# Down weights issued by ScalarE instead of SyncE in a hybrid decoder's mixture of experts

## The reference

```python
def moe_ffn(x, norm_ffn, w_router, b_router, w_gu, b_gu, w_down, b_down):
    xn = rms_norm(x, norm_ffn)
    logits = xn @ w_router + b_router
    top_v, top_e = lax.top_k(logits, 4)              # 4 of 32 experts
    gates = jax.nn.softmax(top_v, axis=-1)
    ...
    h = xn[tok] @ w_gu[e] + b_gu[e]                  # (rows, 1024) @ (1024, 2048)
    gate = jnp.minimum(h[:, :1024], 7.0)
    up = jnp.clip(h[:, 1024:], -7.0, 7.0)
    y = ((up + 1.0) * gate * jax.nn.sigmoid(1.702 * gate)) @ w_down[e] + b_down[e]   # (rows, 1024) @ (1024, 1024)
    ...
    return x + out                                   # y added at its tokens, times the gate
```

## Time and profile before

| | |
|---|---|
| median of 3 runs | 1318.44 us (1316.54 to 1318.85) |
| time of the profiled execution | 1316.15 us |
| its span | 1314.3 us |
| PE busy | 1235.2 us, 94% of the span |
| DMA, mean over the span | 352 GB/s |
| of the two queues of the run: issued by SP / by ACT | 460.42 MB / 1.05 MB |
| granted TensorE clock, mean | 0.993 |

### The profile page before, as it was taken

One profiled execution on the slowest core, in us unless ns is written; L12 is line 12 of the kernel. 1 busy time (PEld: TensorE's weight loads), 2 busy tenths in 40 slices (PEclk: granted clock), 3 DMA queues, 4 the chain that ended last, 5 costly groups with the idle time before them and its releaser, 6 DMA issues.

```text
span 1314.3 us, 17102 instructions
## 1 busy us (share of the span) xinstructions
PE 1235.2 (94%) x6632; PEld 576.2 (44%) x6632; DVE 350.1 (27%) x887; ACT 221.5 (17%) x479; POOL 16.6 (1%) x27
## 2 busy tenths in 40 slices
PE   7999999999899999899898989999999998989998
PEld 4556778766433433333332433333434333333332
DVE  2552455415461212111221212122111221211113
ACT  2123234300431111111111111011111111111110
POOL 0000000001100000000000000000000000000000
PEclk9999989999899999999999999999999999999999
DMA  9684642487369999999999999998999999999994
GB/s 334 174 247 151 227 126 73 105 289 297 128 269 429 429 428 428 427 429 429 428 428 429 428 428 428 428 377 356 429 427 430 429 428 428 430 428 428 430 427 201
DMA packets 76531, 462.15 MB, mean 352 GB/s; under 512 B 19282, under 2 KB 34370, under 8 KB 51650
## 3 DMA queue, kind: packets, MB, share of 16 engines
q1 hardware_dynamic: 71874, 460.42, 86.4%
q10 hardware_dynamic: 4608, 1.05, 0.4%
HBM read 458.48 MB, written 5.07 MB: 353 GB/s over the span
## 4 chain that ended last, share of the span: by engine, by line
PE 56%; DMA 39%; DVE 2%; ACT 2%; issue 1%; SPq 0%; DVEq 0%; ACTq 0%
DMA arena<-w_down 37%; PE banks L1241 12%; PE banks L1168 11%; PE banks L2027 6%; PE banks L585 5%; PE banks L527 2%; PE banks L763 2%; PE banks L1362 2%; PE banks L1198 2%; DMA arena<-w_gu 2%; PE banks L1147 1%; PE banks L1107 1%; PE banks L639 1%; PE banks L2046 1%; PE banks L544 1%; PE banks L652 1%
## 5 line engine op out<-in xcount | busy, mean ns | idle before, releaser
L1168 PE MATMUL banks<-arena 128*64 128x512 f32 x1984 | 442.5, 596 | 28.1 <-DMA arena<-w_gu 28.1
L1168 PEld LDWEIGHTS banks<-arena 128*64 128x64 f32 x1984 | 138.5, 137 | 303.8 <-issue 240.3
L1241 PE MATMUL banks<-arena 128*64 128x512 f32 x1056 | 236.4, 594 | 12.6 <-DMA arena<-w_down 12.5
L1298 DVE TENSOR_SCALAR arena<-banks 128x512 f32<-128x512 f32 x33 | 22.8, 692 | 475.2 <-PE banks L1168 446.7
L1241 PEld LDWEIGHTS banks<-arena 128*64 128x64 f32 x1056 | 73.7, 137 | 156.6 <-issue 121.1
L1271 ACT ACTIVATE arena<-arena 128x512 f32<-128x512 f32 x33 | 20.8, 630 | 542.0 <-DVE arena L1298 542.0
L1324 DVE TENSOR_TENSOR arena<-banks,arena 128x528 f32<-128x528 f32 x64 | 45.3, 708 | 176.6 <-PE banks L1147 176.6
L2027 PE MATMUL banks<-arena 128*128 128x512 f32 (+1 forms) x192 | 79.0, 569 | 0.0
L585 PE MATMUL banks<-arena 128*128 128x264 f32 x256 | 62.3, 398 | 0.5 <-ACT arena L804 0.5
L1147 PE MATMUL banks<-arena 128*128 128x264 f32 x256 | 61.2, 392 | 0.0
L1267 ACT COPY arena<-banks 128x512 f32<-128x512 f32 x33 | 19.3, 586 | 220.9 <-PE banks L1129 220.8
(11 more groups left out here) (348 smaller groups left out, 931.0 us busy)
## 6 DMA issues: line engine op xcount, KB each, us to landing
arena<-w_gu SPq DMA_DIRECT2D x128, 2048.0 KB, 23.9
arena<-w_down SPq DMA_DIRECT2D x64, 2048.0 KB, 24.7
arena<-w_in SPq DMA_DIRECT2D x8, 2048.0 KB, 11.3
arena<-cache_moba_k SPq DMA_DIRECT2D x16, 256.0 KB, 2.9
arena<-cache_moba_v SPq DMA_DIRECT2D x16, 256.0 KB, 2.7
arena<-w_out SPq DMA_DIRECT2D x2, 2048.0 KB, 12.7
arena<-w_in SPq DMA_DIRECT2D x2, 1024.0 KB, 9.2
arena<-cmp_w_k SPq DMA_DIRECT2D x1, 2048.0 KB, 10.4
```

Of the source, the lines that this page charges most:

```text
L1168: mm = nc.tensor.matmul(banks[64 * x:64 * x + 64, BG + b, :], xgT[:, c % 4, 64 * (c // 4):64 * (c // 4) + 64], w[:, D * b + 512 * x:D * b ...
L1241: mm = nc.tensor.matmul(banks[64 * x:64 * x + 64, BY, :], product[:, c, 64 * part:64 * part + 64], w[:, 512 * x:512 * x + 512], start=Fals ...
```

## The change

In the experts' stage the down loads of 29 of the 32 experts (all but the first and the last two) are no longer issued by SP but by ACT. ACT issues the two down loads of expert q, `load_down(act, ..., q)`, in one go right after `keep_out` of pass q-1, that is, behind the copies of the down products whose end frees the two slots. SP keeps the gate/up loads in their order. The waits on `half_down` and `ydone` move with the loads; on ACT they are already met when it comes to them, since `keep_out` waited for `ydone`. Nothing of the arithmetic, the buffers or PE's order changes.

```diff
@@ experts_sp
             load_gate_up(sp, sp.value_load(order_i[0:1, 2:3], min_val=0, max_val=NEXP - 1), 2)
-            load_down(sp, 1, 1)
             with sp.Fori(2, TWICE) as q:
                 load_gate_up(sp, placed_expert(sp, q + 1), q + 1)
-                load_down(sp, placed_expert(sp, q), q)
...
-            load_down(sp, sp.value_load(order_i[0:1, TWICE:TWICE + 1], min_val=0, max_val=NEXP - 1), TWICE)
             with sp.Fori(TWICE + 2, NEXP - 1) as q:
                 load_gate_up(sp, placed_expert(sp, q + 1), q + 1)
-                load_down(sp, placed_expert(sp, q), q)
@@ experts_act
+            def step_and_load(q, half, scattered):
+                step(q, half, scattered)
+                load_down(act, placed_expert(act, q), q)
...
             step(1, 1, 0)
+            load_down(act, 1, 1)
             step(2, 0, None)
+            act.wait_ge(l_listed, 1)
+            load_down(act, act.value_load(order_i[0:1, 2:3], min_val=0, max_val=NEXP - 1), 2)
             with act.Fori(1, TWICE // 2 - 1) as k:
-                step(2 * k + 1, 1, k)
-                step(2 * k + 2, 0, None)
+                step_and_load(2 * k + 1, 1, k)
+                step_and_load(2 * k + 2, 0, None)
             step(TWICE - 1, 1, TWICE // 2 - 1)
+            load_down(act, act.value_load(order_i[0:1, TWICE - 1:TWICE], min_val=0, max_val=NEXP - 1), TWICE - 1)
             keep_rows(act, TWICE + 1)
             keep_rowsT(act, TWICE + 1, xgT_twin)
             sigmoid(act, TWICE)
             keep_out(act, TWICE - 1, 1, None)
+            load_down(act, act.value_load(order_i[0:1, TWICE:TWICE + 1], min_val=0, max_val=NEXP - 1), TWICE)
             keep_productT(act, TWICE)
...
             keep_out(act, TWICE, 0, TWICE // 2)
             keep_out(act, TWICE + 1, 1, None)
+            load_down(act, act.value_load(order_i[0:1, TWICE + 2:TWICE + 3], min_val=0, max_val=NEXP - 1), TWICE + 2)
             keep_rowsT(act, TWICE + 3)
             keep_productT(act, TWICE + 2)
             with act.Fori(TWICE // 2 + 1, PAIRS - 1) as k:
-                step(2 * k + 1, 1, k)
-                step(2 * k + 2, 0, None)
+                step_and_load(2 * k + 1, 1, k)
+                step_and_load(2 * k + 2, 0, None)
```

## The result

The changed kernel takes 1340.89 us (median of 4 runs, 1338.66 to 1343.28) against 1317.49 before: 23.4 us more, a ratio of 1.0175, 95% interval 1.0163 to 1.0188. The profiled execution took 1338.66 us, with a span of 1336.9.

What follows compares the result with a forecast made beforehand. The DMA was taken to bound two stretches, 578 us together, PE the part between. Terms 14.6 + 5.2 + 4.4 = 24.2 us on the profiled 1316.15 gave 1340.4, by the median 1342.6; forecast 1341, range 1320 to 1353.

Steps and rivals of the forecast that it cites:

- DMA-bound stretches: 488.65 to 807 and 1027.88 to 1287 us: DMA stays full, a pair of passes still takes 58.7 us.
- Two queues in place of one, packet by packet: Experts' loads: queues alternate by 16 KB packets, each getting half while both have work; the largest term, 14.6 us.
- my layout: Schedule of a pair of DMA-bound passes with both queues sharing the DMA: cycle closes at 58.7 us, PE lags.
- The lag, 7.3 us at each end: At each DMA-bound stretch's end, before the double pass and at kernel end: PE 7.3 us later, 14.6 in all (0 to 19.6).
- Where PE waits: DMA-bound passes: no longer at many places for w_down, but 3 to 5 us at a late gate/up part of odd passes.
- the landing of the second down load at 23.2: In the laid-out pair of passes: down loads issued at 3.6 us land at 13.4 and 23.2.
- Later issue, "this alone costs nothing there": DMA-bound stretches: down loads issued 8 and 3.6 us later cost nothing, as a load waits 25 us for its turn.
- ACT's time, 4.4 us: Written-out part: issues and register load, 1.45 us, delay copies PE waits for at three places; 4.4 us (4.2 to 6.0).
- The first down part at the double pass, 5.2 us: After 886 to 888 us: ACT issues at 894.1 instead of SP's 888.89, 5.2 us more idle DMA (0 if hidden).
- The order hardly suffers: Rival, experts' loads: nearly PE's order is kept, only ACT's 4.4 us or nothing remains, 1318 to 1326 us; chance 0.18.
- Two queues move more bytes: Rival, DMA-bound stretches: one queue's packets fill the other's gaps, 1308 us or anything under 1315.8; chance 0.10.
- The clock: Rival, TensorE: longer PE waits drop the clock, lag grows 3.4 us at both ends, 1348 to 1354 us; chance 0.10.

Runs made afterwards that it cites:

- e8: The changed kernel with the down weights in rows of 4 KB instead of 16 KB, gate/up still 16 KB: 1577.71 us, ratio 1.199.
- e4: The changed kernel with ACT issuing the down loads of passes 1 to 15 only, SP those from pass 16 on: 1327.07 us, ratio 1.0063.
- e5: The changed kernel with SP issuing the down loads up to pass 15, ACT those from pass 16 to 30: 1330.89 us, ratio 1.0097.
- e6: The changed kernel with ACT issuing only the second down load of each pass, SP keeping the first in its order: 1327.43 us, ratio 1.0073.
- e11: The changed kernel once more, unaltered, in the same rounds as e10: 1338.8 us, ratio 1.0164 to the kernel before.
- e1: The kernel before, all loads on SP's queue, both down loads issued only after the second down part is used: 1318.96 us, ratio 1.0004.
- e12: The changed kernel with ACT issuing the first down load right when that part is used, ahead of its three copies: 1331.92 us, ratio 1.0118.
- the halves: The two runs with one half of the change each, e4 and e5: ratios 1.0063 and 1.0097 to the kernel before.
- e10: The changed kernel, ACT in the loops holding its down loads until the next pass's third gate/up part has landed: 1362.53 us, ratio 1.0347.

## Why the prediction was right, point by point

The forecast of 1341 us was met by 1340.89. That closeness owes much to chance: the terms summed to 24.2 us, in the profiles they make 20.1, and they were off by 2 to 4 us in both directions.

*DMA-bound stretches.* Right: 29.37 us a pass before and after, the rate unchanged.

*Two queues in place of one, packet by packet.* Right where both have work: in the five us from 741 q1 moved 1.05 MB and q10 1.10, and e8 shows that packets are counted and not bytes (228 to 235). Here the Trainium skill's rule (DMA: Bandwidth & Descriptors, Queues, rings and completion order) and the trace agree. But my layout had both at work all the time, and SP's queue ran empty at times. Its load of 697.23 landed 14.6 us later, at 711.8; the next was issued only at 711.77, when PE had used the slot, and its first packet came at 715.18. In between q10 had the DMA to itself (the last two rows are the us from 711):

```profile
697.23 0.33 SPq L383 DMA_DIRECT2D arena<-w_gu  x1
...
arena<-w_gu SPq DMA_DIRECT2D x1, 2048.0 KB, 14.6
...
711.77 0.33 SPq L383 DMA_DIRECT2D arena<-w_gu  x1
...
q10 hardware_dynamic: 24, 0.39, 91.8%
q1 hardware_dynamic: 4, 0.00, 0.2%
```

*The lag, 7.3 us at each end.* The mechanism is shown by e4, e5 and e6. The size about held once a low clock is taken off. The first lag measured 7.4 us in the profile of after, 9.6 in e4 and 10.2 in e11, which runs the same instructions up to there. In e4 and e11 PE's last wait ahead of the double pass was a long one (4.8 and 3.2 us), and the 16 matmuls behind it took 5.95 and 5.15 us instead of 3.65; without that 7.3 and 8.7 are left. The second lag is the 9.4 us that PE needs more after the last load. Of these 2.5 are the same thing behind PE's last wait, at 1248.53 (6.11 us instead of 3.65, rows below): from there on PE waits for no load, so nothing covers them. Another 1.6 are the low clock at 1316 to 1318 us (the 16 transposes of L1677 took 3.50 instead of 1.91 us). That leaves 5.3; in e5 and e11, with the full clock behind the last wait, it was 6.2 and 5.6.

*Where PE waits.* Wrong. I had three us at the fourth gate/up part of odd passes; the trace has up to 5.7 us at the second down part, the longest ones all in even passes, where I had about 1 us. The step that failed is the landing of the second down load at 23.2. In the pass with the wait at 1248.53 ACT issued at

```profile
1225.08 0.35 ACTq L383 DMA_DIRECT2D arena<-w_down  x1
...
1225.60 0.34 ACTq L383 DMA_DIRECT2D arena<-w_down  x1
```

and the second load landed at 1248.48. PE had ended the down products at 1222.99, so the landing is at 25.5, although the issue was at 2.6 and not at 4: the first packet came 3.5 us after the first issue. I had let the two loads move at half the rate, one behind the other, from the issue on.

*Later issue, "this alone costs nothing there".* True on one queue (e1). In the changed kernel it costs about 0.5% (e12 against e11), a term the sum did not have. The sentence held for a load that waits 25 us for its turn, and the change takes just that wait away.

*ACT's time, 4.4 us.* Too high: 0.6 us. The three copies came 0.0, 0.3 and 0.4 us later. The register load and the issues ran beside the copies ahead of them; I had put them in line behind.

*The first down part at the double pass, 5.2 us.* Too high. ACT's issue at 902.32 came 4.3 us later than SP's at 888.89, each counted from the second pass and less the first lag. Of the 10.7 us of the last load's later landing, less 7.4, 3.3 are left, ACT's 0.6 among them (3.9 in e5, 4.2 in e11).

Together 7.4 + 9.4 + 3.3 = 20.1 us in the profile. The median's 23.4 is 3 us more. Of these 1.8 us lie ahead of the second pass, in stages that the change doesn't touch, and 0.6 behind the last scatter. The second series (e11) gives 20.8, the halves 21.7. Why the later runs of one kernel differ by this much stays open.

*The rivals.* "The order hardly suffers" is out by e4, e5, e6 and e8. "Two queues move more bytes" is out: 428 GB/s as before. The clock came in part. The mean fell from 0.993 to 0.974, and after the longest waits the 16 matmuls that followed took up to 6.5 us for 3.65, as here in the changed kernel, where the granted clock was 0.83 from 1240 to 1260 us:

```profile
1240.34 3.60 PE L1241 MATMUL banks<-arena 128*64 128x512 f32 x16
1248.53 6.11 PE L1241 MATMUL banks<-arena 128*64 128x512 f32 x16 [4.58 <-DMA arena<-w_down]
```

Within a stretch the pass of 29.37 us shows that PE's time to spare covered it. At the ends it adds to the lags what is said above; that is read from the rows, no run held the clock up. The rule of the Trainium skill (TensorE: Matmul & The Clock Gate, Part 1), that an idle array falls back to the half rate, agrees with these rows.

## What to carry to other kernels

When one queue feeds a ring and the DMA is the bound, the order of the queue is worth as much as its rate: a second queue is served beside it, packet for packet, and delivers early what is wanted late. Nothing is lost while the DMA stays full, so look for the cost where the bound changes sides and at the end of the kernel, where PE has to work off what came too early and nothing covers a low clock behind its last long wait. A deep queue hides late issues, a short second one doesn't; whoever splits loads over two queues should issue them at the first moment at which the slot is free.

## What the runs showed of the hardware that was not expected

- How long a load issued by ACT took to its first DMA packet depended on what SP had under way. In the 20 passes of the changed kernel with two of SP's loads issued and not landed it was 2.9 to 3.6 us from the first issue, in the 9 with one or none 1.0 to 2.1 us. In e10 it was 1.0 to 1.9 us with one, in e12 3.4 to 3.6 us with two or three. Why is not shown.
- ACT's queue of instructions issues a DMA while copies ahead of it in the program still run or have not begun (issue at 733.45, copies from 733.28 and from 733.88).
- Packets of 4 KB for a third of the bytes cost 1.5% of the rate (29.82 against 29.37 us a pass), and 256 packets of 16 bytes a pass cost 0.16 us of it.
